# One change in three parts to a four-layer transformer kernel: split fp32r passes in two projection stages, plain early expert tiles, a product moved into a norm

## What is computed (the reference, cut)

```python
# layers 0 and 1
mod = silu(c) @ ada_w[l] + ada_b[l]                  # six vectors of 1024; mod_c from c_ctx
h, hc = x * (1 + sc1) + sh1, xc * (1 + csc1) + csh1
p = concat([hc, h]) @ w_in                           # layer 0: 1536 columns, layer 1: 2816
#   layer 0: q, k with rms norm and rotary positions, v, and a pooling branch
#   layer 1: differential attention (q, k rotated) and a gated convolution of 31 taps
y = concat([attention, branch]) @ w_out              # layer 0 also for the context
x = layer_norm(ALPHA * x + g1 * y)
x = layer_norm(ALPHA * x + g2 * swiglu(x * (1 + sc2) + sh2, ffn_in, ffn_out))
# layers 2 and 3
z = x @ w_in                                         # mlstm or rglru, and cross attention to a memory
x = layer_norm(ALPHA * x + mix @ w_out)
q = x @ w_q                                          # 8 heads, two halves of 128
s = q . subkeys ; top 16 of each half, top 16 of the 256 sums, softmax -> weights of 128 experts a token
y = sum over chosen e of weight_e * gelu(x . u_e) * v_e     # 16384 experts
x = layer_norm(ALPHA * x + y)
```

## Time and profile before

| what | value |
|---|---|
| runs before | 3397.36, 3400.22, 3401.0 us |
| the profiled execution's own time | 3395.68 us |
| its span, first to last instruction | 3393.9 us |
| mean granted TensorE clock | 0.966 of full |
| layer 0 projection stage | 42.9 to 168.5 us of the span |
| layer 1 projection stage | 760.4 to 909.4 |
| norm of `hidden00`, then `out01` | 497 to 537 |
| early expert tiles, layers 2 and 3 | 1461 to 1781, and the same in layer 3 |

### The profile page before, as it was taken

One profiled execution on the slowest core, in us unless ns is written; L12 is line 12 of the kernel. 1 busy time (PEld: TensorE's weight loads), 2 busy tenths in 40 slices (PEclk: granted clock), 3 DMA queues, 4 the chain that ended last, 5 costly groups with the idle time before them and its releaser, 6 DMA issues.

```text
span 3393.9 us, 53499 instructions
## 1 busy us (share of the span) xinstructions
PE 3141.2 (93%) x20608; PEld 2718.7 (80%) x20608; DVE 2142.6 (63%) x3792; ACT 1298.7 (38%) x1960; POOL 111.4 (3%) x135
## 2 busy tenths in 40 slices
PE   6978998999979999697999999999798899999998
PEld 2548988986759978487999999887588899999886
DVE  1376556553466530569986666784559996666686
ACT  1144435431244421332554444433442454444433
POOL 0020000000000000013000000000003100000000
PEclk8989999999989998799999999999899999999999
DMA  7703543547215533033566655674234466665664
GB/s 286 265 6 112 186 161 125 186 149 251 85 50 174 185 132 118 31 122 121 212 239 224 212 204 205 227 242 142 78 118 137 174 225 234 204 223 207 216 238 136
DMA packets 190527, 580.74 MB, mean 171 GB/s; under 512 B 16768, under 2 KB 61824, under 8 KB 185504
## 3 DMA queue, kind: packets, MB, share of 16 engines
q1 hardware_dynamic: 185120, 541.04, 46.2%
q10 hardware_dynamic: 4608, 33.56, 2.4%
q0 software_dynamic: 640, 4.00, 0.3%
HBM read 543.92 MB, written 34.60 MB: 170 GB/s over the span
## 4 chain that ended last, share of the span: by engine, by line
PE 82%; DVE 11%; ACT 3%; DMA 2%; issue 1%; ACTq 0%; DVEq 0%; SPq 0%; POOL 0%; POOLq 0%
PE ps L949 29%; PE ps L990 26%; PE ps L821 4%; PE ps L776 4%; PE ps L939 3%; PE ps L1205 3%; DVE w_split L1968 2%; PE ps L824 2%; PE ps L913 1%; ACT arena L1471 1%; PE ps L976 1%; DVE arena L1741 1%; PE ps L898 1%; PE ps L715 1%; DVE arena L2181 1%
## 5 line engine op out<-in xcount | busy, mean ns | idle before, releaser
L1968 DVE TENSOR_TENSOR w_split<-ring,w_split 128x1024 fp32r<-128x1024 f32 x747 | 914.3, 1226 | 589.3 <-ACT w_split L1532 588.4
L949 PE MATMUL ps<-x_split,w_split 128*128 128x256 f32 x9312 | 1196.6, 287 | 58.2 <-DVE w_split L1968 44.6
L949 PEld LDWEIGHTS ps<-x_split,w_split 128*128 128x128 f32 x9312 | 1167.7, 194 | 84.6 <-issue 44.5
L1532 ACT ACTIVATE w_split<-ring 128x1024 fp32r<-128x1024 f32 x747 | 788.7, 1058 | 748.0 <-PE ps L990 441.9
L990 PE MATMUL ps<-w_split,h_split 128*128 128x512 f32 x3864 | 914.1, 390 | 2.6 <-DVE w_split L1968 2.6
L990 PEld LDWEIGHTS ps<-w_split,h_split 128*128 128x128 f32 x3864 | 712.7, 188 | 143.3 <-issue 2.9
L1602 ACT ACTIVATE arena<-ps 128x256 f32<-128x256 f32 (+1 forms) x256 | 98.6, 385 | 460.2 <-PE ps L949 458.5
L821 PE MATMUL ps<-arena,ring 128*128 128x512 f32 (+1 forms) x416 | 153.8, 524 | 12.6 <-DVE arena L2344 6.1
L821 PEld LDWEIGHTS ps<-arena,ring 128*128 128x128 f32 x416 | 80.5, 195 | 76.0 <-issue 68.0
L776 PE MATMUL ps<-x,ring 128*128 128x256 f32 (+1 forms) x608 | 132.2, 379 | 3.5 <-ACT x L1505 3.5
L776 PEld LDWEIGHTS ps<-x,ring 128*128 128x128 f32 (+1 forms) x608 | 108.4, 179 | 26.8 <-issue 4.3
(11 more groups left out here) (272 smaller groups left out, 2434.3 us busy)
## 6 DMA issues: line engine op xcount, KB each, us to landing
ring<-in_peer_u SPq DMA_DIRECT2D x256, 512.0 KB, 3.3
ring<-in_peer_v SPq DMA_DIRECT2D x256, 512.0 KB, 4.2
ring<-in_ffn_in SPq DMA_DIRECT2D x132, 512.0 KB, 3.2
ring<-in_ada SPq DMA_DIRECT2D x96, 512.0 KB, 6.3
ring<-in_ffn_out SPq DMA_DIRECT2D x66, 512.0 KB, 3.2
spread_rows<-arena ACTq DMA_DIRECT2D x32, 1024.0 KB, 3.9
arena<-spread_rows SPq DMA_DIRECT2D x20, 1536.0 KB, 8.3
ring<-in_pq SPq DMA_DIRECT2D x32, 512.0 KB, 3.2
```

What stands on the lines that cost most here:

```text
L949: last = mm(dst, w_split[:, w, wp, at:at + P], rhs[rp], start=(first and i == 0), stop=(final and i == 2), skip_group_check=shared)
L1532: f(w_split[0:rows, w, 0, :], ring[0:rows, slot, :], ACT.Copy).then_inc(w_high, 1)
L1968: v.tensor_tensor(w_split[0:rows, w, 1, :], ring[0:rows, slot, :], w_split[0:rows, w, 0, :].bitcast(F32), ALU.subtract).then_inc(w_low, 1)
```

## The change

1. In layers 0 and 1, the feature-form tiles from tile 1 (layer 0) and tile 2 (layer 1) on are done as split passes: k = 0 to 6 as three fp32r passes from `w_split`, k = 7 plain from the ring. That is tiles 1 to 7, 10 and 11 in layer 0, and 2 to 15 in layer 1. ScalarE makes the high part of tile n + 2 directly behind its copy of tile n, waiting for that block to be filled; VectorE makes the low part at the head of a step. The input (k = 0 to 6) is split before the tiles, in layer 1 the context's half between tiles 1 and 4.
2. In layers 2 and 3, twenty early expert tiles (0; 16 to 23; 24, 27, ..., 54) are plain, and their high and low parts are not made.
3. The latent output product of layer 0 begins inside the last norm of the context: its tile 0 between the mean and the variance matmuls, the parts of its tiles 1 and 2 behind the squares (ScalarE) and behind the centring (VectorE). The stage borders between `hidden00` and `out01` are gone.

```diff
+PLAIN = [u for u in range(AHEAD) if u < 1 or QUERIES <= u < QUERIES + U_PICK or QUERIES + U_PICK <= u < QUERIES + U_PICK + U_SPREAD and u % 3 == 0]
+PLAIN_PRODUCTS = {0: 1, 1: 2}
+def split_products(l):
+    return [n for n, (_, _, _, form) in enumerate(project_tiles(l)) if form == FEATURES and n >= PLAIN_PRODUCTS[l]]
...
+        def low_part(k):
+            if k < PHASES:
+                return h_split[:, k, :, :]
+            return w_split[:, SPLIT - 1, :, :].rearrange("p i (k t) -> p (i k) t", t=T)[:, 2 * (k - PHASES):2 * (k - PHASES) + 2, :]
...
+                def split_product(n, b):                      # TensorE
+                    pe.wait_ge(w_low, split0 + at + 1)
+                    pe.wait_ge(early_out, out0 + n - 1)
...
+                    for k in range(KD - 1):
+                        if at == 0:
+                            pe.wait_ge(parts_low, (KD - 1) * l + k + 1)
...
+                        for i, (wp, rhs) in enumerate(((0, high), (0, low), (1, high))):
+                            mm(whole, w[wp], rhs, start=(k == 0 and i == 0), stop=False)
+                    k = KD - 1
+                    last = mm(dst, ring[:, b[0], k * P:(k + 1) * P], hT[:, k, t0:t0 + nt], start=False, stop=True)
+                    last.then_inc(block_used, 1)
...
-            def norm(name):
+            def norm(name, between=None):                     # TensorE
                 last.then_inc(ln_mean, 1)
+                if between:
+                    between()
...
+                def early_in(u, blk):
+                    if u in PLAIN:
+                        plain_in(u, blk)
+                    else:
+                        go_in(u, u % 2, blk, w_base + splits_to(u) + 1)
...
+                def product_high(n):                          # ScalarE
+                    at, seq = splits.index(n), product_block(l, n)
+                    act.wait_ge(filled[seq % R], 16 * (seq // R + 1))
+                    if at >= 2:
+                        act.wait_ge(block_used, product_block(l, splits[at - 2]) + 1)
+                    f(w_split[:, at % 2, 0, :], ring[:, seq % R, :], ACT.Copy).then_inc(w_high, 1)
...
                     f(proj[:, j, 0:nt], pair[:, n % 2, 0:nt], ACT.Copy).then_inc(early_out, 1)
+                    product_high(n + 2)
+                    if l == 1 and 1 <= n <= 4:
+                        input_high((CTX,), 2 * n - 2, min(2 * n, KD - 1))
                     if l == 0 and n < len(ROPE[0]):
                         act.wait_ge(early_out, n + 1)
...
+                norm(name, s, l, 2, between=(lambda: out_highs(f"out0{LAT}", out_tiles(0, LAT), 1, SPLIT)) if crossed else None)
...
                 for i in range(len(ROPE[l])):                 # VectorE
+                    product_low(i + 2 if l == 0 and i < 7 else i + 3 if l == 0 else i + 6)
...
+                    norm(f"hidden{l}{s}", s, l, 2,
+                         prepare=(lambda: out_lows(f"out0{LAT}", out_tiles(0, LAT), 1, SPLIT)) if crossed else None)
```

More of the change, by code:

```diff
@@ L158, with splits_to @@
 READ, WRITE = 12, 16
+def splits_to(u):
+    return u - sum(p < u for p in PLAIN)
 def project_weights(l, tensor, n_products):
@@ L966, in one @@
                     last.then_inc(block_used, 1)
-                for i in range(len(tiles)):
+                for i in range(lo, hi):
                     place.steps(pe, 1, 1, lambda _, par, b: one(i, par, b))
-                n_tile[0] += len(tiles) - 1
-                norm(name)
-            def norm(name):
+                if hi == len(tiles):
+                    n_tile[0] += len(tiles) - 1
+                    norm(name)
+            def norm(name, between=None):
                 for k in range(KD):
@@ L1043, in hidden @@
                 turn_back(by_token_at[True])
-                norm(name)
-                leave()
+                norm(name, between)
+                if between is None:
+                    leave()
             def turn_back(by_token):
@@ L1229, in first_query_and_input @@
                             query_last.then_inc(block_used, 1)
-                        input_last = passes(ps[:, 4, 0:T], b[1][3], k * P, [x_split[:, i, k, :] for i in range(2)],
-                                            k == 0, k == KD - 1)
+                        input_last = mm(ps[:, 4, 0:T], ring[:, b[1][0], k * P:(k + 1) * P], x[:, LAT, k, :],
+                                        start=(k == 0), stop=(k == KD - 1))
                     input_last.then_inc(block_used, 1)
-                    n_split[0] += 1
                 place.steps(pe, 1, 2, lambda _, par, b: first_query_and_input(b))
+                split_ready(KD - 1)
+                n_split[0] += 1
                 score(0)
@@ L1505, in shifted, with norm @@
                 f(x[:, s, k, :], res[:, k, :], ACT.Identity, bias=param(f"ln{ln}b{k12}", k)).then_inc(ln_x, 1)
-            def norm(name, s, ln, k12, follow=None, prepare=None):
+            def norm(name, s, ln, k12, follow=None, prepare=None, between=None):
                 if prepare:
@@ L1532, in high_of, with out_highs @@
                 f(w_split[0:rows, w, 0, :], ring[0:rows, slot, :], ACT.Copy).then_inc(w_high, 1)
-            def out_highs(name, tiles):
-                place.at = first_block(name) + 1
-                for i in range(1, len(tiles)):
+            def out_highs(name, tiles, lo=1, hi=None):
+                place.at = first_block(name) + lo
+                for i in range(lo, hi or len(tiles)):
                     tile, rows = tiles[i]
@@ L1722, in _ @@
                 out_highs(f"out{l}{LAT}", out_tiles(l, LAT))
-                norm(f"out{l}{LAT}", LAT, l, 1, "split", lambda: (ahead(l, 0), ahead(l, 1)))
+                norm(f"out{l}{LAT}", LAT, l, 1, "split", lambda: ahead(l, 1))
                 peer(l)
@@ L1785, in project_early @@
                     rotate(l, len(ROPE[0]) - 1)
+                    product_low(11)
                     biased(1, 0)
@@ L1939, in norm, with out_lows @@
                 n_ln[0] += 1
-            def out_lows(name, tiles):
-                place.at = first_block(name) + 1
+            def out_lows(name, tiles, lo=1, hi=None):
+                place.at = first_block(name) + lo
                 base = split_before(name)
-                for i in range(1, len(tiles)):
+                for i in range(lo, hi or len(tiles)):
                     tile, rows = tiles[i]
@@ L2388, in _ @@
                 plain_sum(f"out{l}{LAT}")
-                norm(f"out{l}{LAT}", LAT, l, 1, "split", lambda: (early_low(l, 0), early_low(l, 1)))
+                norm(f"out{l}{LAT}", LAT, l, 1, "split", lambda: early_low(l, 1))
                 peer(l)
```

149 lines of the change are left out of this document (116 added, 33 removed).

## The result

The changed kernel takes 3411.11 us in the median of 12 runs (3406.63 to 3425.55), the kernel before 3400.55 beside it. One of the 12 runs of the kernel before took 6138.17 us and is not in the ratio. The ratio is 1.004, 95% interval 1.003 to 1.005. The profiled execution took 3411.53 us, its span is 3409.8 and its mean granted clock 0.964.

What follows compares the result with a forecast made beforehand. TensorE, with 82% of the chain, was taken to bound the kernel. Terms +19.7, -6.9, -3.2 and -6.0 summed to +3.6: 3399.3 us for an execution like the profiled one, 3404 for the median; 8 in 10: 3387 to 3419.

Steps and rivals of the forecast that it cites:

- The forecast case: Whole kernel: no change within 0.2% (3393.4 to 3407.0 us), chance 0.43.
- its alternative: Whole kernel: slower by more than 0.2%, chance 0.33, the case of Rival A.
- My own signs: Layer 0's stage ends near 187, tile 10 starts about 12 behind tile 9; wrong if before 175 or clock under 0.9.
- Part 1a: Layer 0's projection: ScalarE's wait for blocks delays root, reciprocal and low; +19.7 us (13 to 29).
- with the change tile 7 ends 8.7 later: Layer 0's projection: two tiles take 24.4 us, one 12.2 against 10.2 before, carried through with the ring's order.
- The tile-10 term: Layer 0's projection: tile 10 starts 12.6 us after tile 9's end and not 3.3, so 9.3 lost.
- Part 1b: Layer 1's projection: six wide tiles gain 7.4 us, narrow ones cost 0.5; sum -6.9 (-9 to -3).
- so the narrow tiles gain nothing: -1 to +2: Layer 1's eight narrow tiles: two take 9.9 to 10.6 us against steps of 5.1; +0.5 taken for the input splits.
- Part 2: Expert tiles of layers 2 and 3: first spread 4.9 us earlier, spread steps +3.8; both layers -3.2 (-13 to +5).
- Part 3: Border between hidden00 and out01: tile 3 starts at 516.8 where it was 522.9; -6.0 us (-7 to -3.5).
- Rival A: Layer 0's projection, tiles 3 to 7: clock falls in TensorE's waits, +10, 3414 us, up to 3419; chance 0.33.
- Rival B: Layer 0's projection: ScalarE's wait does not decide, layer 0 gains 5 to 10, total 3377; milder form 3389; together 0.24.

Runs made afterwards that it cites:

- the run with the late high: Changed kernel with layer 0's high parts made behind square, root and kept modulation piece: 3393.45 us; under layer 1, high parts behind sigmoid and kept piece there: 3406.46 us.
- the run with both late: Changed kernel with, in layer 0, ScalarE's high part behind the root and VectorE's low part at the end of its step: 3387.9 us, ratio 0.9975.
- the filled run: Changed kernel with products without use filling TensorE's idle time ahead of waits in layer 0: 3411.5 us, ratio 1.0032.

## Why the prediction was right and wrong

**The forecast case was wrong, its alternative right in sign.** I took no change (within 0.2%) as the likeliest; it came out slower by 0.4% [0.3, 0.5], 7 us above the point and inside the range. That it lies so near is luck. All four terms were off, three up and one down: by stages it is +30.0 for +19.7, +1.9 for -6.9, -7.3 for -3.2, -3.8 for -6.0. They add up to +20.8 for +3.6, and the first two lie outside the ranges that I gave them. Stages that the change does not touch gave 4.9 back in this profile, which no term of mine foresaw, and the medians differ by only 10.6, since the profiled execution of before was 4.5 to 4.9 under its median.

**My own signs.** The stage of layer 0 ends near 199 and not 187, its reciprocal starts 12.2 us behind a tile's end (87.05 to 99.22) as forecast, and tile 10 starts 13.8 behind the end of tile 9 for some 12. Its granted clock is 0.85, and I had written that I am wrong if it is under 0.9: the forecast named TensorE's waits and priced the clock behind one of them alone. Layer 1's stage takes 151 us, not 142.

**Part 1a, layer 0: the mechanism was right, its size was not.** Square and root behind the wait, the reciprocal late, the low behind it, the hole at tile 10 through the biased step: each is in the rows above, and the run with the late high shows that the order is the cause (19.9 of 30.0 us), and the run with both late that VectorE's order is most of the rest (6.3). The failed step is "with the change tile 7 ends 8.7 later": it ends at 140.5, 17.1 later than the 123.4 of before. A part of the miss is arithmetic: the working had two tiles in 24.4, and three such pairs from the end of tile 1 at 60.5 end at 133.7, which is 10.3 later and not 8.7. From tile end to tile end they took 26.5, 26.5 and 27.0 (60.5, 87.0, 113.5, 140.5), which is 6.8 us above three times 24.4. More than half of that is the clock: with the idle time filled these six tiles take 4.0 less. The rest is spread: high parts start 10.0 and 10.1 behind the ends of tiles 3 and 5 for the 9.7 that I used, and the turn of a finished piece waits for the kept piece behind the root (1.74 at 126.12), where I had counted only its work, 0.5. The tile-10 term, 9.3, measured 10.4 (from the start of tile 8 to that of tile 10 the shift grows from 17.0 to 27.4). What stands behind it, +2.4 for tile 11, -2.5 for both tiles' passes and +1.8 for the clock, was +1.7 and measured +2.5.

**Part 1b, layer 1: the failed step is "so the narrow tiles gain nothing: -1 to +2".** The wide tiles gave 7.1 for 7.4. The narrow ones cost 9.0 in this profile, about 6 in the others. I compared two tiles of 9.9 to 10.6 with two steps of 5.1 and took the difference as nothing. The upper end alone, 0.4 over eight tiles in pairs, is 1.6. The rows show two more things that the working left out: the wait ahead of the kept piece, with a table load of 1.28 us on ScalarE ahead of it (TensorE idle 3.73 at 815.47), and the lower clock, 0.90 in that stretch for 0.96 before. The run with the late high puts ScalarE's order at 2 to 3.4; how the rest is shared out stays open.

**Part 2, experts: too careful.** First spread 4.9 earlier: measured 5.4, counted from the second query tile, and in layer 2 1.5 more at the norm and tile 0. The spread steps +3.8: measured +3.0, slack included. The range for both layers, -13 to +5, held -7.3. Undoing tiles 16 to 23 cost 12.6 us in the total, so they are worth 5.4 to 6.3 in each layer.

**Part 3, the border.** Tile 3 starts as I worked it out: 544.12, where the shift of 27.75 and my 516.8 give 544.6. What failed is what follows: five tiles take 17.1 us for the 14.5 of before, since TensorE had waited 3.16 us and the granted clock was 0.69 from 541 to 552. So -3.8, not -6.0. The term put the clock behind this wait at nothing. In the run with both parts late the same wait of 3.16 us is followed by a granted clock of 1.00 (520 to 531), the five tiles take 14.6 and the border comes to -6.4 (33.89 for 40.26), so the order of work was priced rightly; in four other profiles it is -4.9.

**Rival A** had the right side, and its reason holds in part. The clock did fall in tiles 2, 3, 5 and 7, more than the two that it asked for. It costs at least the 4.1 us of the filled run; the tiles themselves are 7.1 us longer by it, not 10. Without it the change would still lose in this stage, and layer 1's narrow tiles, which Rival A does not have, are the other half of the miss. **Rival B** is refuted: with ScalarE's wait behind the root, and nothing else moved, 19.9 of the 30.0 us are gone. The rule of the Trainium skill, "TensorE: Matmul & The Clock Gate", section "Back-to-back issue gap", does not hold for these passes: the wide tiles' gain of 7.1 in six is that of the row's 0.227 us, and not the 19.6 by the rule's 131 ns.

## What to carry to other kernels

An instruction that waits for a transfer belongs behind everything on its engine that others need sooner, not ahead of it: here one line moved on ScalarE and one on VectorE were worth 26 us of 30. Before a product is split in parts, ask for each tile when its block lands: where it lands just in time for a plain product, high and low come on top, and the cheaper product loses; there leave it plain (164.80 for 173.31 in layer 0). And when the terms of a change are estimated, test them one by one, since a total within 0.4% hid pieces of +30, +9, -7, -7 and -4.

## What was not expected of the hardware

The same instructions get a different clock in different kernels, and that is worth as much as a part of the change. Attention of layer 0 has the same instructions in all kernels. Its first 45 us, before, changed, and with the filler (the clock is the third number from the end):

```profile
169.50:214.50 45.00, 32.73 (x204) 18.61 (x204) 36.42 (x80) 21.45 (x80) 21.53 (x21) 0.77 0.04 12
```

```profile
199.50:244.50 45.00, 30.43 (x212) 17.68 (x212) 37.60 (x84) 21.46 (x80) 21.51 (x21) 0.85 0.04 12
```

```profile
196.40:241.40 45.00, 36.89 (x178) 21.11 (x180) 31.68 (x70) 17.69 (x69) 21.50 (x21) 0.54 0.04 12
```

From the first scores to the mean of `out00` they take 122.0, 119.5 and 125.7 us; with the late high (clock 0.58) it is 127.3, which took back 7.8 of the 19.9 us won in the stage before it. Here it repeats: the six profiles of kernels that are the same up to the end of this stage have 119.3 to 119.7 us. What decides it the runs do not show.

Other stretches differ from one profile to the next with the same instructions. The first 192 matmuls of layer 3's projection take 44.45 us after a wait of 3.50 us in the changed kernel, 41.65 after the same wait in the one before, and 41.65 to 44.5 in the others. The border takes 35.4 us in three of the kernels that are the same up to it and 36.5 in two. So a stage behind a wait has an uncertainty of some microseconds that belongs to no edit, and a single profile should be read by stages.

The waits ahead of which the clock fell in layer 0 were short: 2.33 and 1.04 us ahead of tile 5, and 1.74, 1.61 and 1.04 ahead of tile 7; at the border 3.16. With the idle time filled the clock is at its full level from 98 to 137, so it is the idle time that brings it down there.
